# Gated input's units in four of six places, expert loads regrouped, and the next stage's first two units split within the last pair of experts

## What is computed

```python
for i in range(DEPTH):                       # DEPTH = 2
    ...                                      # i = 0: s5 and pooling, i = 1: stick-breaking attention
    x = layer_norm_2(DEEPNORM_ALPHA * x + mix, ln_mix_g[i], ln_mix_b[i])
    ple = (p[i] @ ple_w_proj[i]) * jax.nn.sigmoid(x @ ple_w_gate[i])
    ffn = grouped_moe(x, router_w, router_bias, moe_w1[i], moe_w3[i], moe_w2[i])
    x = layer_norm_2(DEEPNORM_ALPHA * x + ffn + ple, ln_ffn_g[i], ln_ffn_b[i])

def grouped_moe(...):
    ...                                      # scores, group choice, top 2, gates
    h = jax.nn.silu(jnp.einsum('td,edf->etf', xt, w1)) * jnp.einsum('td,edf->etf', xt, w3)
    h = h * gates.T[:, :, None].astype(h.dtype)
    y = jnp.einsum('etf,efd->td', h, w2)
```

## Time and profile before

| | us |
|---|---|
| median of three runs | 1730.63 |
| lowest, highest | 1729.23, 1730.76 |
| the profiled execution | 1729.61 |
| its span in the trace | 1727.7 |
| TensorE busy | 1669.3 (97%) |
| VectorE busy | 945.7 (55%) |
| ScalarE busy | 640.0 (37%) |
| moved by DMA | 419.72 MB |

### The profile page before, as it was taken

How to read it: one execution, slowest core, us unless ns; L and a number is a source line. 1 busy time by engine, 2 the same in 40 slices (tenths; PEclk the granted TensorE clock), 3 DMA queues, 4 the chain that set the end, 5 groups by cost and what they waited for, 6 DMA issues and landing times.

```text
span 1727.7 us, 20825 instructions
## 1 busy us (share of the span) xinstructions
PE 1669.3 (97%) x8496; PEld 1199.8 (69%) x8496; DVE 945.7 (55%) x1319; ACT 640.0 (37%) x834; POOL 63.4 (4%) x91
## 2 busy tenths in 40 slices
PE   8999999999999999999999999999997999999996
PEld 6888887878888888878887887744433777744332
DVE  4755687675465645876676598611114667611114
ACT  4643445364424443453454364311112344311110
POOL 1000001000000000003000000000000000000000
PEclk9999999999999999999999999999999999999998
DMA  7555540655555554615755354899999544799995
GB/s 305 190 182 188 197 168 25 230 184 187 180 198 191 192 189 168 207 69 186 246 178 168 138 207 156 307 429 428 428 427 412 200 146 147 311 430 426 426 427 241
DMA packets 47366, 419.72 MB, mean 243 GB/s; under 512 B 5345, under 2 KB 5345, under 8 KB 9137
## 3 DMA queue, kind: packets, MB, share of 16 engines
q1 hardware_dynamic: 43776, 405.82, 61.9%
q0 software_dynamic: 3504, 12.68, 2.1%
HBM read 417.43 MB, written 1.05 MB: 242 GB/s over the span
## 4 chain that ended last, share of the span: by engine, by line
PE 86%; DMA 5%; DVE 5%; ACT 3%; issue 0%; SPq 0%; DVEq 0%; ACTq 0%
PE hh L1324 11%; PE y L681 11%; PE y L683 10%; PE y L682 10%; PE hh L681 9%; PE hh L683 9%; PE hh L682 9%; DMA wide<-pairs 4%; PE hh L1356 3%; PE turn L1356 3%; PE turn L1228 2%; PE y L1367 1%; DVE w_lo L1956 1%; DMA raw<-units 1%; PE turn L803 1%; PE y L967 1%
## 5 line engine op out<-in xcount | busy, mean ns | idle before, releaser
L1956 DVE TENSOR_TENSOR w_lo<-raw,w_hi 128x2048 fp32r<-128x2048 f32 x193 | 438.1, 2289 | 142.7 <-ACT w_hi L1503 142.0
L1503 ACT ACTIVATE w_hi<-raw 128x2048 fp32r<-128x2048 f32 x193 | 365.1, 1912 | 65.1 <-DMA raw<-units 64.9
L681 PE MATMUL hh<-w_hi,xt_hi 128*128 128x512 f32 x704 | 279.4, 397 | 2.3 <-DVE w_lo L1956 1.2
L683 PE MATMUL hh<-w_hi,xt_lo 128*128 128x512 f32 x704 | 274.9, 391 | 0.0
L682 PE MATMUL hh<-w_lo,xt_hi 128*128 128x512 f32 x704 | 274.6, 390 | 0.0
L681 PE MATMUL y<-w_hi,xt_hi 128*128 128x512 f32 (+1 forms) x464 | 182.5, 393 | 3.3 <-DVE xt_lo L2057 3.1
L683 PE MATMUL y<-w_hi,xt_lo 128*128 128x512 f32 (+1 forms) x464 | 178.4, 385 | 0.0
L682 PE MATMUL y<-w_lo,xt_hi 128*128 128x512 f32 (+1 forms) x464 | 178.4, 384 | 0.0
L1324 PE MATMUL hh<-wide,work 128*64 128x512 f32 x688 | 154.0, 595 | 11.7 <-DMA wide<-pairs 11.7
L681 PEld LDWEIGHTS hh<-w_hi,xt_hi 128*128 128x128 f32 x704 | 132.3, 188 | 31.1 <-DVE xt_lo L2057 2.9
L683 PEld LDWEIGHTS hh<-w_hi,xt_lo 128*128 128x128 f32 x704 | 132.2, 188 | 28.1
(11 more groups left out here) (383 smaller groups left out, 1853.6 us busy)
## 6 DMA issues: line engine op xcount, KB each, us to landing
raw<-units SPq DMA_DIRECT2D x193, 1024.0 KB
wide<-pairs SPq DMA_DIRECT2D x61, 2048.0 KB
extra<-pairs SPq DMA_DIRECT2D x12, 2048.0 KB
xt_wide<-pairs SPq DMA_DIRECT2D x12, 2048.0 KB
wide<-pairs SPq DMA_DIRECT2D x8, 1024.0 KB
late<-pairs SPq DMA_DIRECT2D x5, 1024.0 KB
raw<-pairs SPq DMA_DIRECT2D x5, 1024.0 KB
spare<-pairs SPq DMA_DIRECT2D x2, 2048.0 KB
```

Of the source, the lines that this page charges most:

```text
L681: pe.matmul(dst, left[0], right[0], start=start, stop=False)
L683: return pe.matmul(dst, left[1], right[0], start=False, stop=stop)
L1503: act.activation(hi[r][:, :], raw[r][:, :], ACT.Copy).then_inc(hi_ready, 1)
L1956: dve.tensor_tensor(lo[r][:, :], raw[r][:, :], hi[r][:, :].bitcast(F32), ALU.subtract)\
```

## The change

It has two parts.

*Places and ring.* A new helper `place(q)` gives a unit's place. The last unit of each gated input (171, 192) goes to the place of the unit three before it, so the gated input uses four places and not five. It is therefore loaded after the second unit of the gated input is used, and not before the stage. Units 172 and 173 change places. The ring's buffers are cut anew: buffers for loads 2 to 5 take two neighbouring places each, those of loads 7 and 8 one place's `raw` and `late`, so their loads are two DMAs of 1 MB. Their waits change: for the stage that begins after unit q - 1, loads 2 and 3 by halves after units q - 7 and q - 6 (before: q - 6 and q - 5), load 8 after q - 5 (before: q - 1), loads 4 and 5 by halves after q - 3 and q - 2 (before: both whole after q - 3), load 7 after q - 1 as before. On ScalarE the split of the gated input's last unit moves behind the wait for the fourth unit.

*Next stage's units.* Unit 172 is requested when load 40 is used (before: 42), 173 when 42 is, 175 to 177 when 44 is, and 174, last, when 47 is. ScalarE splits 172 in the last pair between silu and the copy of the turned activations, 173 right behind that copy, and 174 after load 47 is used. VectorE does its part for both behind its multiplication (2679). `next_input` is no longer called there; `low_xt(0)` alone is.

```diff
-            for r in range(MOE_RING):
-                a0, a1 = ((q + 2 * (r // 2) + k) % RAW + RAW * (r % 2) for k in range(2))
...
+            pairs_at = [[(q + of + k) % RAW + RAW * upper for k in range(2)] for of in (5, 3) for upper in range(2)]
+            pairs_at += [[(q + of) % RAW + RAW * upper for upper in range(2)] for of in (2, 1)]
+            for r, (a0, a1) in enumerate(pairs_at):
...
+        def place(q):
+
+            if q - BEFORE_MOE[0] in (0, 1):
+                return (2 * BEFORE_MOE[0] + 1 - q) % RAW
+            return (q - 3 if q + 1 in BEFORE_MOE else q) % RAW
...
                 for part in range(2):
-                    sp.wait_ge(unit_used, q - 5 + part)
+                    sp.wait_ge(unit_used, q - 6 + part)
                     for k in (2, 3):
                         load_wide(l, k, (part,))
-                for k, free in ((4, q - 2), (5, q - 2), (6, q - 1), (7, q), (8, q)):
-                    sp.wait_ge(unit_used, free)
-                    load_wide(l, k)
+                sp.wait_ge(unit_used, q - 4)
+                load_wide(l, 8)
+                sp.wait_ge(unit_used, q - 3)
+                load_split(q - 1, q - 1)
+                for part in range(2):
+                    sp.wait_ge(unit_used, q - 2 + part)
+                    for k in (4, 5):
+                        load_wide(l, k, (part,))
+                load_wide(l, 6)
+                sp.wait_ge(unit_used, q)
+                load_wide(l, 7)
...
+            q = BEFORE_MOE[0]
+            for n_, p, i in ((0, PAIRS - 2, 4), (1, PAIRS - 1, 0), (3, PAIRS - 1, 2), (4, PAIRS - 1, 2), (5, PAIRS - 1, 2),
+                             (2, PAIRS - 1, 5)):
+                wait_used(sp, 0, p, i)
+                load_split(q + n_, q + n_)
...
-                if n_ < RAW:
-                    wait_used(sp, 0, PAIRS - 1, (0, 2, 5)[n_ // 2])
-                else:
-                    sp.wait_ge(unit_used, q - RAW + 1)
+                sp.wait_ge(unit_used, q - RAW + (2 if n_ == RAW else 1))
...
-                split_to(PLE_UNITS)
                 act.activation(x_high[:, :, :], x[:, :, :], ACT.Copy).then_inc(x_high_ready, 1)
                 for j in range(2):
                     wait_units(2 * j + 2)
+                    if j == 1:
+                        split_to(PLE_UNITS)
...
-                    wait_used(act, l, PAIRS - 1, 3)
+                    wait_used(act, l, PAIRS - 1, 5)
                     split()
...
-            def split_freed(l):
-
-                wait_used(act, l, PAIRS - 1, 1)
-                for _ in range(2):
-                    split()
+            def split_freed(l, unit):
+
+                wait_used(act, l, PAIRS - 2 + unit, 4 - 3 * unit)
+                split()
...
                     act.activation(silu, h_bank[0][:, :], ACT.Silu).then_inc(silu_ready[l], 1)
+                    if not next_ and l < DEPTH - 1:
+                        split_freed(l, 0)
...
                     act.activation(turned.rearrange("p k s -> p (k s)"), h_bank[0][:, :], ACT.Copy).then_inc(turned_ready[l], 1)
+                    if not next_ and l < DEPTH - 1:
+                        split_freed(l, 1)
...
-                    if not next_ and l < DEPTH - 1:
-                        split_freed(l)
...
+                    if not next_ and l < DEPTH - 1:
+                        split(2)
                     for c, src in enumerate((h_bank[1], turn_bank[1])):
...
-                    next_input()
+                    low_xt(0)
                     dve.wait_ge(moe_out, l + 1)
```

More of the change, by code:

```diff
@@ L333, in program @@
             ring.append([])
-            for r in range(MOE_RING):
-                a0, a1 = ((q + 2 * (r // 2) + k) % RAW + RAW * (r % 2) for k in range(2))
-                if (q + 2 * (r // 2)) % RAW == RAW - 1:
-                    a0, a1 = ((RAW - 1, RAW), (2 * RAW - 1, 0))[r % 2]
+            pairs_at = [[(q + of + k) % RAW + RAW * upper for k in range(2)] for of in (5, 3) for upper in range(2)]
+            pairs_at += [[(q + of) % RAW + RAW * upper for upper in range(2)] for of in (2, 1)]
+            for r, (a0, a1) in enumerate(pairs_at):
                 ring[l].append(nc.alloc_sbuf_tensor_at(f"wide{l}_{r}", [P, 2 * UNIT], F32, offset=STREAM_AT + 4 * UNIT * a0)
@@ L363, in load_split @@
             def load_split(q, row):
-                sp.dma_start(raw[q % RAW][:, :], a["units"][row]).then_inc(unit_loaded[q % RAW], 32)
+                sp.dma_start(raw[place(q)][:, :], a["units"][row]).then_inc(unit_loaded[place(q)], 32)
             for q in range(RAW):
@@ L404, in _ @@
             load_rounds(rounds - 5, rounds)
-            for q in range(rounds * RAW, BEFORE_MOE[0]):
+            for q in range(rounds * RAW, BEFORE_MOE[0] - 1):
                 if q == BEFORE_MOE[0] - 4:
@@ L411, in _ @@
             load_experts(0)
-            for q in range(BEFORE_MOE[0], BEFORE_MOE[1]):
+            q = BEFORE_MOE[0]
[3 more added lines that the diff above has]
+                load_split(q + n_, q + n_)
+            load_wide(1, 1)
+            for q in range(BEFORE_MOE[0] + RAW, BEFORE_MOE[1] - 1):
                 n_ = q - BEFORE_MOE[0]
-                if n_ == RAW:
-                    load_wide(1, 1)
                 if n_ == STICK_UNITS + 2:
@@ L691, in unit @@
             def unit(k):
-                s = n[0] % RAW
+                s = place(n[0])
                 n[0] += 1
@@ L1500, in split @@
                 for _ in range(times):
-                    r = n[0] % RAW
+                    r = place(n[0])
                     act.wait_ge(unit_loaded[r], seen(unit_loaded[r], 32))
```

## The result

The changed kernel takes **1743.9 us** (median; 1740.73 to 1746.39), the kernel before beside it 1729.88 (1729.16 to 1730.76): ratio 1.0079, 95% interval 1.0070 to 1.0089. It is 0.8% slower, 14.0 us, where 6.9 us were predicted and 1741.5 was the upper end of the range. The profiled execution took 1744.37 us with a span of 1742.7, 15.0 us more than before, so nearly all of the loss can be read in it. It also spreads over 5.7 us where the kernel before spreads over 1.6.

The account below looks back on a forecast made before the run. Expert stages end when their DMA load stream ends. First stage and transition 7.36 + 1.3 - 1.1 = +7.56, second stage -0.63, together +6.9 us on the 1730.63 median: 1737.6 us, range 1733.5 to 1741.5.

Parts of the forecast that it names:

- The last pair: First expert stage's end: unit 172 lands behind load 47, its split delays ScalarE's copy, +7.36 us on the path, advance included.
- the split doesn't hold ScalarE: Rival, first stage's last pair: unit 172 lands by about 1315.5, so the copy isn't late; 1728.3 us, chance 0.08.
- The split in the gated input: Both stages: ScalarE's split of the last unit, ahead of the last two sigmoids, lies wholly on the path, 1.91 us.
- rival of half clock at this gather: TensorE's 2.2 us of idling near 1110 and 1496 bring half clock, 1.7 us each: 1741.0 us, chance 0.08.
- The ring's advance: Expert stages' loads: buffers filled earlier gain 2.55 us, less the 1.91 us split, leaving 0.64 us (second stage 0.63).
- the stream would be 2.55 us earlier: Expert stage's start: load 9 lands at 1129.1 + f, not 1131.6 + f; TensorE's use of load 1 limits more.
- earlier by a unit: Ring of expert buffers: the change was read as moving halves of loads 4 and 5 earlier by a unit.
- The transition: Between the expert stages: later TensorE start and later second turn, less half clock that goes: -1.1 us, bounds -1.7 and +0.6.
- 1345.4, +0.6: Between the stages: the second row tile's turn, before at 1344.77, comes from TensorE at 1345.4, 0.6 us later.
- the half clock after 1345.6 should go: Between the stages: TensorE no longer waits before the second row tile's turn, so 1.7 us of half-clock cost goes.
- Half clock in the down projection: First stage's last pair: after 8.6 us of TensorE idling, half clock costs 0 to 1.7 us, taken +1.3.
- The rule that I weighed: DMA queue: completion isn't first in, first out per issuing engine, but each DMA engine takes its ring in order.

Follow-up runs that it names:

- e4: The kernel before, old ring and order of units kept, with only the splits of units 172 and 173 moved into the last pair: 1736.3 us, ratio 1.0033.
- e3: e2 with the split of the gated input's last unit moved ahead of the wait for the fourth unit: 1727.05 us, ratio 0.9981.
- e5: The changed kernel with the split of the gated input's last unit moved ahead of the wait for the fourth unit: 1738.81 us, ratio 1.0048.
- e2: e1 with ScalarE's split of unit 174 moved behind the table load and xt_hi: 1731.92 us, ratio 1.0012.
- e6: The kernel before with the loads of ring buffers 7 and 8 always issued as two requests of 1 MB: 1731.06 us, ratio 1.0005.
- e8: The changed kernel with ScalarE's split of unit 174 moved behind the table load and first xt_hi: 1737.37 us, ratio 1.0046.
- e10: The changed kernel with 18 matmuls without use in TensorE's gap ahead of the first stage's last down projection: 1741.39 us, ratio 1.0067.
- e7: The changed kernel with 36 matmuls without use in TensorE's gap ahead of the first stage's last down projection: 1748.39 us, ratio 1.0103.
- e1: The changed kernel with the splits of units 172 and 173 put back behind the last pair on both engines: 1735.05 us, ratio 1.0027.
- e9: e3 with ScalarE's splits between its two roundings of the last pair's results and behind them, VectorE's likewise: 1727.28 us, ratio 0.9982.

## Why the prediction was wrong in size

The direction, the place and the waits that the change adds were right; the size was half. Four terms of the sum failed, by 7.9 us together: the stream up to load 45 (3.1 us too low), the transition (2.1), the half clock ahead of the gated input (not in the sum, 1.8) and the half clock in the down projection (1.0). The shift of the profiled execution can be added up along the path, start to start, from the rows of both:

| term | predicted | measured |
|---|---|---|
| up to the gated input's last sigmoids (half clock at 1072) | 0 | +1.84 |
| split ahead of the sigmoids, first stage | +1.91 | +1.80 |
| stream up to load 45, first stage | -2.55 | +0.53 |
| load 45 to the down projection | +8.00 | +8.00 |
| half clock in the down projection | +1.3 | +2.26 |
| transition | -1.1 | +0.96 |
| second stage, all | -0.63 | -0.4 |
| sum | +6.9 | +15.0 |

(In the order of the rows: 1108.48 - 1106.64; 2.11 - 0.31; 195.58 - 195.05; 14.84 - 6.84. The down projection is the shift of the request of unit 174 after, 172 before, at the stage's end, 1344.20 - 1329.77 = 14.43, less the 12.17 of the four rows above. The transition is the shift at the second stage's gated input, 1508.02 - 1492.63 = 15.39, less 14.43. The second stage is the span's 15.0 less 15.39. The prediction's 7.36 is 1.91 - 2.55 + 8.00.)

- *The last pair.* Right to the hundredth, if by luck: the prediction had +7.36 with 0.64 of advance in it, so 8.00 at a fixed load 45. Unit 172 came behind every pair load. The rival "the split doesn't hold ScalarE" is out: TensorE had nothing to do from 1322.15 on (8.68 us before 1330.83), so a split of 1.91 us would have had to start by about 1320.2, and the unit landed at 1328.30, 8 us too late. e4 shows the term alone.
- *The split in the gated input.* Right in both stages. The prediction's working even said that the unit lands about 1102, before ScalarE is free (in e3 it had landed by 1104.18); e3 and e5 show that one line, the wait ahead of the split, made the whole price. The rival of half clock at this gather did not come in the changed kernel; in e2 it came once, in the second stage.
- *The ring's advance.* The step "the stream would be 2.55 us earlier" was mis-sized by 3.1 us in the first stage, +0.53 for -2.55. The late share took 2.2 of them: I had reckoned a load's time as bytes by rate, and not as its slowest share. The other 0.9 is advance that was not there. Without a late share it is 1.8 us in the first stage and 2.2 in the second; the two requests for one, 0.6 and 0.2 us in e6, are enough to explain that. A reading of the change was wrong as well: the halves of loads 4 and 5 don't come "earlier by a unit". Their first halves are requested where they were and their second halves a unit later (SP's four requests take from 1102.43 to 1109.28, before two from 1100.60 to 1101.43). No run tests it alone.
- *The transition.* The step "1345.4, +0.6" failed. The second row tile's turn starts 17.25 us behind the last unit's request (1344.20 to 1361.45), before 15.00 (1329.77 to 1344.77): +2.25. Of the 1.65 us too few, 0.75 lie ahead of TensorE's start, since the unit took 5.22 us to land and not 4.74, and the way from there to xt_lo was 0.3 us longer. The other 0.9 are the clock's. I had put 1.3 us on the half clock behind this wait; in the changed kernel it holds for the first 12 matmuls, 4.90 us or 2.1 over their full-clock time. The step "the half clock after 1345.6 should go" held in the main: the turn no longer waits, the stretch is gone, and from it to the second gated input 1.3 us were gained of 1.7. e2 (3.1 us) and e8 (5.0 us in the trace) show what the wait for unit 174 is worth.
- *Half clock in the down projection.* I took 1.3 out of 0 to 1.7, from stretches of 3.4 us in the kernel before. The stretch here begins in the wait and lasts to 1335.3, 4.5 us of it under TensorE's work. e10 shows 2.25 us.
- *Half clock ahead of the gated input.* Not in the sum, and not shown to be of the change's making. The wait ahead of it ends 0.45 us later than before (1073.54 and 1073.09, as does e6's with the old ring, 1073.57), which is part of the 1.84. The wait is 3.66 us (3.39 in the kernel before), while the stretch behind it lasts 3.4 us in the kernel before, e2, e3, e4, e6, e7, e8 and e10, and 6.8 in the changed kernel, e1, e5 and e9. The long one comes in four of nine profiles with the new ring's early loads and in none of three with the old ring, so it varies between kernels that are alike up to there, and whether these loads have part in it can't be said from so few. 1.84 us of the profiled difference are its; what share of the 14.0 us between the medians, one profile a kernel can't say.

The range was too narrow because I bounded three terms (the late share, two stretches of clock) by what one profile of the kernel before shows: no lag, and stretches of 3.4 us. In the profiles of this case the lag goes from 0 to 2.5 us and the stretches behind TensorE's new waits of 4.9 us and more last 6.8 or 10.2 us. The unprofiled executions fit this: of the changed kernel's six, the fastest (1740.73 us) has a mean granted clock of 0.993 and the slowest (1746.39 us) 0.989. What made the clock differ there is not known.

The rule that I weighed, of the Trainium skill, page "DMA: Bandwidth & Descriptors", section "Queues, rings and completion order": by its second half the forecast held. The trace shows shares out of order, and whole loads in order. In the changed kernel the first shares of unit 172 landed at 1324.05, ahead of the last share of load 47 at 1325.82, which had been requested before it; the unit as a whole was complete at 1328.30, behind load 47. That each engine kept its own order fits this but isn't shown, since the trace doesn't name the engines. The overtaking was worth no more than the late share's 2.2 us.

## To carry over

Before a step that waits for a load is put in front of another on an in-order engine, ask when the load lands, not when it is requested: behind this kernel's full queue a request that came 7.5 us earlier bought nothing. The same split can be free or cost its full length by the side of one wait on which it stands, so look for an engine's idle time at a moment when the data are there. When a change lets TensorE wait longer at one place, price the clock behind that wait by more than the stretch seen behind a shorter one: the old kernel's 3.4 us stood behind waits of 2.8 and 3.4 us, and behind the changed kernel's waits of 5.1 and 8.7 us the stretches were 6.8 and 10.2. And measure two parts of a change together as well as apart: what one gives back (here VectorE's 2.0 us) the other can take away.

## What was unexpected

- One of a load's 16 shares can land 1.8 to 2.5 us behind the others up to the end of an expert stage, where the other fifteen land within some 2 us of one another; a load's users wait for the last share.
- Waits of 3.4 to 3.7 us ahead of the gated input were followed by 3.4 us at a granted clock of 0.50 in some executions and by 6.8 us in others. A wait of 2.2 us ahead of the stick-breaking stage's first unit was followed by full clock in the kernel before, e2 and e3, and in e6, whose waits are those of the kernel before, by a stretch of 6.8 us (from 1337.8).
- 36 filler matmuls on 128x256 float32 appear as 72 rows and take 15.71 us; 18 take 7.94.
